# A decoder block on one core: high and low activations side by side in one matmul, the down projection with tokens stationary, one-hots built on GpSimd

## The reference, cut to what matters

```python
def block_fn(args):                      # 64 tokens at a time
    s1 = einsum('thd,kd->thk', qb[..., :half], k1); s2 = ...      # 128 keys each
    v1, i1 = top_k(s1, 16); v2, i2 = top_k(s2, 16)
    cand, cand_idx = v1[:, None] + v2[None], i1 * 128 + i2        # 256 of each head
    top, pos = top_k(cand, 16); idx = cand_idx[pos]               # 8 heads x 16 experts
    g = softmax(top)
    act = gelu(einsum('thkd,td->thk', u_tab[idx], hb)) * g
    return einsum('thk,thkd->td', act, v_tab[idx])
x = x + gt_f * rms_norm(ff, g_post_ffn)
```

## Time and profile before

| | |
|---|---|
| three runs, median (lowest to highest) | 2189.06 us (2187.78 to 2191.6) |
| the profiled execution | 2194.0 us |
| its span in the profile | 2192.2 us |
| busy: PE, PEld, DVE, ACT, POOL | 92%, 86%, 72%, 40%, 10% |
| granted TensorE clock, mean | 0.987 of 2.4 GHz |
| transfers | 618 MB, 282 GB/s on average |
| `w_lo` (L354), `w_hi` (L678) | 544 each, 1223 and 1059 ns |

### The profile page before, as it was taken

One profiled execution on the slowest core, in us unless ns is written; L12 is line 12 of the kernel. 1 busy time (PEld: TensorE's weight loads), 2 busy tenths in 40 slices (PEclk: granted clock), 3 DMA queues, 4 the chain that ended last, 5 costly groups with the idle time before them and its releaser, 6 DMA issues.

```text
span 2192.2 us, 40118 instructions
## 1 busy us (share of the span) xinstructions
PE 2017.2 (92%) x15446; PEld 1880.2 (86%) x15446; DVE 1578.6 (72%) x2251; ACT 868.2 (40%) x1272; POOL 208.5 (10%) x145
## 2 busy tenths in 40 slices
PE   5999999989999999998888888899999999999997
PEld 4888884449999999998888888898998998998996
DVE  4668997658778878866888888666666666666665
ACT  3012223025444434445555555433343333343333
POOL 0000000000000000001222222111111111111110
PEclk9999999989999999999999999999999999999999
DMA  8996666978856676666999999877777778877874
GB/s 348 422 411 242 235 231 259 393 293 309 300 167 211 209 241 213 208 197 236 339 337 339 338 337 338 316 286 287 281 279 284 283 276 285 292 266 286 293 269 147
DMA packets 135962, 618.15 MB, mean 282 GB/s; under 512 B 16049, under 2 KB 24785, under 8 KB 99025
## 3 DMA queue, kind: packets, MB, share of 16 engines
q1 hardware_dynamic: 105984, 464.57, 59.2%
q0 software_dynamic: 18496, 134.24, 16.2%
q10 hardware_dynamic: 11410, 18.36, 2.3%
HBM read 600.26 MB, written 16.79 MB: 281 GB/s over the span
## 4 chain that ended last, share of the span: by engine, by line
PE 56%; DVE 21%; issue 9%; ACT 8%; DMA 5%; DVEq 1%; ACTq 1%; SPq 0%
PE ps L936 17%; PE ps L1263 17%; DVE w_lo L354 6%; ACT w_hi L678 5%; PE ps L974 5%; DVE big L1761 5%; DVE big L1693 5%; PE ps L958 4%; PE ps L1136 4%; PE ps L1085 3%; PE ps L985 3%; ACT oh L791 2%; DVE oh L1686 1%; DVE a_lo L1738 1%; DMA early<-in_w_ada 1%
## 5 line engine op out<-in xcount | busy, mean ns | idle before, releaser
L354 DVE TENSOR_TENSOR w_lo<-raw,w_hi 128x1024 fp32r<-128x1024 f32 x544 | 662.6, 1223 | 448.4 <-ACT w_hi L678 443.9
L678 ACT ACTIVATE w_hi<-raw 128x1024 fp32r<-128x1024 f32 x544 | 576.2, 1059 | 941.8 <-PE ps L1263 452.5
L1263 PE MATMUL ps<-a_hi,w_hi 128*128 128x192 f32 x2048 | 568.7, 278 | 62.8 <-DVE w_lo L354 55.3
L936 PE MATMUL ps<-a_hi,w_hi 128*128 128x192 f32 x2048 | 572.6, 280 | 28.6 <-DVE w_lo L354 24.5
L936 PE MATMUL ps<-a_hi,w_lo 128*128 128x192 f32 x2048 | 565.0, 276 | 0.0
L936 PE MATMUL ps<-a_lo,w_hi 128*128 128x192 f32 x2048 | 565.0, 276 | 0.0
L1263 PE MATMUL ps<-a_lo,w_hi 128*128 128x192 f32 x2048 | 562.9, 275 | 0.0
L1263 PE MATMUL ps<-a_hi,w_lo 128*128 128x192 f32 x2048 | 562.9, 275 | 0.0
L1263 PEld LDWEIGHTS ps<-a_hi,w_hi 128*128 128x128 f32 x2048 | 394.4, 193 | 73.6 <-DVE w_lo L354 66.0
L936 PEld LDWEIGHTS ps<-a_hi,w_hi 128*128 128x128 f32 x2048 | 396.8, 194 | 36.0 <-DVE w_lo L354 27.5
L936 PEld LDWEIGHTS ps<-a_lo,w_hi 128*128 128x128 f32 x2048 | 396.9, 194 | 0.2 <-issue 0.2
(11 more groups left out here) (232 smaller groups left out, 2034.0 us busy)
## 6 DMA issues: line engine op xcount, KB each, us to landing
raw<-in_peer_u SPq DMA_DIRECT2D x256, 512.0 KB, 5.0
raw<-in_peer_v SPq DMA_DIRECT2D x256, 512.0 KB, 4.5
early<-in_w_ada SPq DMA_DIRECT2D x60, 1024.0 KB, 10.5
early<-in_w_front SPq DMA_DIRECT2D x42, 1024.0 KB, 9.2
raw<-in_w_ada SPq DMA_DIRECT2D x20, 1024.0 KB, 10.4
raw<-in_peer_wq SPq DMA_DIRECT2D x32, 512.0 KB, 6.6
big<-in_w_gate_f SPq DMA_DIRECT2D x16, 1024.0 KB, 5.7
raw<-in_w_front SPq DMA_DIRECT2D x14, 1024.0 KB, 8.7
```

The source lines that it names most:

```text
L354: engine.tensor_tensor(w_lo[:, s % 2, part], ring[j % ph.ring][:, part], w_hi[:, s % 2, part].bitcast(F32), ALU.subtract)\
L678: act.activation(w_hi[:, s % 2, :], ring[j % ph.ring], ACT.Copy).then_inc(hi_ready, 1)
L936: done = pe.matmul(ps[:, b % 2, 0:TD], w[:, half, k * P:(k + 1) * P], a[:, kc, 0:TD], start=kc == 0 and m == 0, stop=kc == KC - 1 and m == 2)
L1263: done = pe.matmul(ps[:, c // 2, (c % 2) * TD:(c % 2 + 1) * TD], w[:, j % 2, n * P:(n + 1) * P], a[:, blk, 0:TD], start=i is None and blk ...
```

## The change

In UP, MID and ROUTE `a_hi` and `a_lo` become one tensor `a2`, so that one matmul moves both, 384 columns, against `w_hi`; its second half of the columns collects the product with the low part. `w_lo` by the high part follows with 192 columns. When a block is done, ACT copies the second half of the columns into `stage` (`put_low`), DVE adds the first half from PSUM (`add_block`), and ACT's Gelu then works in place.

In DOWN the activations become stationary and `peer_v` moves, 512 columns at a time, so the output has tokens as rows. Tokens 0 to 127 need a high and a low stationary block; tokens 128 to 191 pack their high and low parts into one block of 128 (`second`). A unit has 10 matmuls. `a_down` lies in `a2`; the low part is written with two instructions. Row sums are made in halves of 1024 columns, one after each unit of even number. At the end `pair` adds high and low rows and the slices of `acc`.

The one-hots are made on POOL, already scaled, eight instructions of 128x128 a group, in the queue in which the gathers stand; DVE's and ACT's steps for them go. The dots are made in halves, and a part of them in MID: 14 rows in MID (5 in its first round, then 3), 50 in ROUTE (8, then 6).

```diff
-USE_FIRST, MASK_FIRST, PUT_FIRST = (5, 7, 9, 11, 13, 15), (5, 7, 9, 11, 13, 15), (7, 9, 11, 13, 15, 15)
+USE_FIRST, MASK_FIRST, PUT_FIRST = (5, 7, 9, 11, 13, 15), (4, 7, 9, 11, 13, 15), (7, 9, 11, 13, 15, 15)
 USE, MASK, PUT = (1, 4, 6, 9, 12, 14), (0, 3, 6, 8, 11, 14), (3, 6, 8, 11, 14, 15)
-DOTS_AT = (1, 2, 4, 5, 7, 9, 10, 12, 13)
-SUMS_AT = (3, 6, 11, 14)
+DOTS_MID_FIRST, DOTS_MID = tuple(range(6, 16)), (1, 4, 6, 9, 12, 14)
+DOTS_ROUTE_FIRST, DOTS_ROUTE = tuple(range(16)), (0, 1, 2, 4, 5, 6, 8, 9, 10, 12, 13, 14)
...
+SUMS_AT = (0, 2, 4, 6, 8, 10, 12, 14)
...
-        a_hi = sb("a_hi", [P, KC, T], F32R)
-        a_lo = sb("a_lo", [P, KC, T], F32R)
+        a2 = sb("a2", [P, KC * 2 * T], F32R)
+        a_pair = a2[:, :].rearrange("p (k m t) -> p k m t", m=2, t=T)
+        a_hi, a_lo = a_pair[:, :, 0, :], a_pair[:, :, 1, :]
+        a_down = a2[:, 0:8 * 2 * TD].rearrange("p (b c) -> p b c", c=2 * TD)
...
-        dots_now = sb("dots_now", [P, len(DOTS_AT)])
-        pair = sb("pair", [P, P])
+        dots_now = sb("dots_now", [P, N_ROUTE_FIRST, 2])
+        pair = sb("pair", [P, TD])
...
-            for n in range(ROWS):
+            v_rows = peer_v.rearrange("b p d -> (b p) d")
+
+            def gather_next(n):
+
+                if n >= ROWS:
+                    return
                 if n >= 3:
                     gp.wait_ge(row_used, n - 2)
                 gather(n, u_rows, got[n % 3], row_in[n % 3])
...
+            def make_masks(g):
+
+                if g == 0:
+                    gp.wait_ge(sel_made, 2)
+                else:
+                    gp.wait_ge(oh_used, g)
+                for t in range(4):
+                    token = slice(4 * g + t, 4 * g + t + 1)
+                    gp.tensor_scalar(masks[:, 0, t, :], iota[:, :], sel_T[:, 0, token], None, ALU.is_equal)
+                    done = gp.tensor_scalar(masks[:, 1, t, :], iota[:, :], sel_T[:, 1, token], sel_T[:, 2, token],
+                                            ALU.is_equal, ALU.mult)
+                done.then_inc(oh_ready, 1)
+            for n in range(3 + ROW_ROUTE_FIRST):
+                gather_next(n)
+            for it in range(PH_ROUTE.n):
+                for j in range(PH_ROUTE.per):
+                    where = MASK if it else MASK_FIRST
+                    for g in range(6):
+                        if where[g] == j:
+                            make_masks(6 * it + g)
+                    halves = DOTS_ROUTE if it else DOTS_ROUTE_FIRST
+                    row0 = ROW_ROUTE + N_ROUTE * (it - 1) if it else ROW_ROUTE_FIRST
+                    if j in halves[1::2]:
+                        gather_next(row0 + halves[1::2].index(j) + 3)
+            for n in (1, 2, 0):
+                gp.wait_ge(row_used, ROWS - (ROWS - 1 - n) % 3)
+                gather(n, v_rows, got[n], v_row_in[n])
...
-            def gelu(b0, i, per):
-
-                whole(b0, i, per)
+            def put_low(b0, i, per):
+
                 b = b0 - B_UP
+                act.wait_ge(split_used, at(i, 2 * per, 2 * b0 + 2))
                 if b % 2 == 0 and (b >= 4 or i is not None):
                     act.wait_ge(gel_out[b // 2 % 2], at(i, 4 * per, 16 * (b // 4)))
-                act.activation(stage[:, b % 4, :], ps[:, b0 % 2, 0:TD], ACT.Gelu).then_inc(gemm_evac, 1)
+                act.activation(stage[:, b % 4, :], ps[:, b0 % 2, TD:2 * TD], ACT.Copy).then_inc(low_put, 1)
+
+            def gelu(b0, i, per):
+
+                b = b0 - B_UP
+                act.wait_ge(summed, at(i, per, b + 1))
+                act.activation(stage[:, b % 4, :], stage[:, b % 4, :], ACT.Gelu).then_inc(gemm_evac, 1)
...
-            def scale_masks(g, i):
-
-                act.wait_ge(oh_masked, at(i, 6, g + 1))
-                for t in range(4):
-                    token = bass.ds(at(i, 24, 4 * g + t), 1)
-                    done = act.activation(masks[:, 1, t, :], masks[:, 1, t, :], ACT.Copy, scale=sel_T[:, 2, token])
-                done.then_inc(oh_ready, 1)
-
...
+                m, per = j // 2, ph.s_per // 2
+                if j % 2 and not (first and m == 0):
+                    put_low(ph.block + m - 1, i, per)
+                if first and m < 2:
+                    return
+                if j % 2 == 0:
+                    gelu(ph.block + m - 2, i, per)
+                elif m % 2 and not (first and m == 1):
...
             def high_group(g, i, made):
 
                 act.wait_ge(at_made, made)
                 b = 4 * (g % 2)
-                act.activation(a_hi[:, b:b + 4, 0:TD], routed_v[:, bass.ds(at(i, 8, 4 * g), 4), :], ACT.Copy)\
+                act.activation(a_down[:, b:b + 4, P:P + TD], routed_v[:, bass.ds(at(i, 8, 4 * g), 4), :], ACT.Copy)\
...
+            def put_second(b):
+
+                act.wait_ge(split_used, PH_DOWN.s_end - 1 + b // 6)
+                act.activation(f_second[:, (b - 4) * 512:(b - 3) * 512], ps[:, b, :], ACT.Copy).then_inc(f_put_act, 1)
...
+            def f_squares(tt, g):
+
+                if tt:
+                    act.wait_ge(f_paired, g + 1)
+                else:
+                    act.wait_ge(split_used, PH_DOWN.s_end - 1 + g // 2)
+                act.activation(squares[:, 4 * tt + g, :], ps[:, 4 * tt + g, :], ACT.Square, accum_out=f_ss[:, tt, g:g + 1])\
                     .then_inc(f_sq, 1)
+
+            put_second(4)
+            put_second(5)
+            f_squares(0, 0)
+            f_squares(0, 1)
+            put_second(6)
+            f_squares(0, 2)
+            f_squares(0, 3)
+            for g in range(4):
+                f_squares(1, g)
...
-                    pe.wait_ge(gemm_evac, at(i, ph.s_per // 2, b - 1))
+                    pe.wait_ge(summed, at(i, ph.s_per // 2, b - 1 - B_UP))
...
-                        for m, (w, a) in enumerate(((w_hi, a_hi), (w_hi, a_lo), (w_lo, a_hi))):
-                            done = pe.matmul(ps[:, b % 2, 0:TD], w[:, half, k * P:(k + 1) * P], a[:, kc, 0:TD],
-                                             start=kc == 0 and m == 0, stop=kc == KC - 1 and m == 2)
+                        cols = slice(k * P, (k + 1) * P)
+                        pe.matmul(ps[:, b % 2, 0:2 * TD].rearrange("p (m t) -> p m t", m=2), w_hi[:, half, cols],
+                                  a_pair[:, kc, :, 0:TD], start=kc == 0, stop=False, skip_group_check=True)
+                        done = pe.matmul(ps[:, b % 2, 0:TD], w_lo[:, half, cols], a_hi[:, kc, 0:TD], start=False,
+                                         stop=kc == KC - 1, skip_group_check=True)
...
-                    for n in range(UCH):
-                        c = (j % 2) * UCH + n
-                        for m, (w, a) in enumerate(((w_hi, a_hi), (w_hi, a_lo), (w_lo, a_hi))):
-                            done = pe.matmul(ps[:, c // 2, (c % 2) * TD:(c % 2 + 1) * TD], w[:, j % 2, n * P:(n + 1) * P],
-                                             a[:, blk, 0:TD], start=i is None and blk == 0 and c % 2 == 0 and m == 0,
-                                             stop=False, skip_group_check=True)
+                    first, low, second = (a_down[:, blk, P:2 * P], a_down[:, blk, 0:P], a_down[:, blk, 2 * P:3 * P])
+                    for tt, a, w in ((0, first, w_hi), (0, low, w_hi), (1, second, w_hi), (0, first, w_lo),
+                                     (1, second, w_lo)):
+                        for n in range(2):
+                            done = pe.matmul(ps[:, 4 * tt + 2 * (j % 2) + n, :], a, w[:, j % 2, n * 512:(n + 1) * 512],
+                                             start=i is None and blk == 0 and w is w_hi and a is not low, stop=False,
+                                             skip_group_check=True)
                     done.then_inc(split_used, 1)
...
-            def turn_out(tt, g):
...
+            pe.wait_ge(v_row_used, ROWS)
+            pe.wait_ge(pair_made, 3)
+            for g in range(4):
+                cols = slice(g * 512, (g + 1) * 512)
+                if g < 3:
+                    pe.wait_ge(f_put_act, g + 1)
+                else:
+                    pe.wait_ge(f_put_dve, 1)
+                pe.matmul(ps[:, 4 + g, :], pair[:, 0:P], acc[:, cols], start=True, stop=False, skip_group_check=True)
+                pe.matmul(ps[:, 4 + g, :], pair[:, TS:TD], f_second[:, cols], start=False, stop=True,
+                          skip_group_check=True).then_inc(f_paired, 1)
...
+                if ph in (PH_UP, PH_MID, PH_ROUTE):
+                    m = j // 2
+                    if j % 2 and (m or i is not None or ph is not PH_UP):
+                        add_block(ph.block - B_UP + m - 1, i, ph.s_per // 2)
+                if ph is PH_MID:
+                    dots_at(j, i, DOTS_MID if i is not None else DOTS_MID_FIRST, ROW_MID, 3)
+                if ph is PH_ROUTE:
+                    dots_at(j, i, DOTS_ROUTE if i is not None else DOTS_ROUTE_FIRST, ROW_ROUTE, 6)
+
+            def add_block(b, i, per):
+
+                dve.wait_ge(low_put, at(i, per, b + 1))
```

(24 more changed lines are left out.)

153 lines of the change are left out of this document (61 added, 92 removed).

## The result

The changed kernel takes 2214.5 us (median of four runs, 2212.5 to 2215.6), the kernel before 2188.4 in the same session: 1.0116 times as long, 95% interval 1.0099 to 1.0134. Forecast were 2064 us, with 1985 to 2135 as the range. The kernel did not become faster but 1.2% slower, which is small but more than the runs scatter, and the time lies outside of the range.

The account below looks back on a forecast made before the run. TensorE was taken to bound UP and MID and to set most of ROUTE and DOWN. UP -12, MID +20, DOWN -104, ROUTE -22 and the end -7 sum to -125, giving 2064 us, range 1985 to 2135.

Parts of the forecast that it names:

- one term of ROUTE: ROUTE, one-hots on POOL: each 128x128 instruction takes 0.35 us, so eight in a group take 2.8 us.
- the port's term: ROUTE: POOL waits out two-input DVE instructions, some five a group, each for half of its 1.14 us: 2.5 us.
- The idle time: ROUTE: POOL waits for DVE's half dot, about 1.1 us after TensorE's use of the group before.
- TensorE's own term in ROUTE: ROUTE: TensorE needs 38.4 us plus 2.5 for 24 one-hot matmuls, 40.9 a round if nothing waits for one-hots.
- the +10 forecast for it: First ROUTE round: all six groups stand two units apart, so it goes from about 53 to 64 us.
- POOL's instructions are dear: Rival in ROUTE: 0.5 us an instruction gives 2124, 0.94 gives 2290; chance 0.13 for 0.45 to 0.7, 0.08 above.
- UP: UP stage: a round falls from 43.7 to 40.7 us, four rounds, -12 us.
- MID: MID stage: three more rows of dots make a round 47.6 us, DVE-bound; +12, first round +8, together +20 us.
- DOWN: DOWN stage: hand-over gives 38.1 us, DVE's pieces 2.8, a round 40.9 instead of 47.4; sixteen rounds, -104 us.
- Transfers: Same bytes in less time: DOWN 327 GB/s, MID 260, ROUTE about 310, against 385 possible; nothing binds, with little room.
- The end: After the last matmul: 12 us of transposing back become about 5 us, -7 us.
- Weight loads: Rival: loads don't hide behind the wide matmul, a unit takes 3.75 us, a round 60, total 2264; chance 0.02.

Follow-up runs that it names:

- the best version: Changed kernel with one-hots back on DVE and ScalarE, a second set of one-hot buffers and two of six groups made a unit earlier: 2041.9 us, 0.9326.

## Why the prediction was wrong

**The step that failed** is one term of ROUTE: "I take 0.35, near the select, since it has the same size and one input but also reads its scalars." It is 0.69. Per group, over the 42 groups of the seven rounds (476.4 us, 11.3 each; forecast 8.0):

| | forecast | measured |
|---|---|---|
| eight instructions | 2.8 | 5.5 |
| behind DVE, and the gather | 2.5 + 1.6 | 3.7 (389.1/42 less 5.5) |
| idle between use and start | 1.1 | 2.1 (87.3/42) |

The price is 2.7 of the 3.3 us that are missing, and the run with half of the instructions puts the forecast's 2.8 in place and comes near the forecast's round. Both halves of the port's term were right: about 0.5 of a DVE piece each (0.59 us of 1.14) and some five in the way. The idle time was short by 1.0, since the gather's dot comes not 1.1 us after the use but only after a high part and a low part that wait for TensorE in turn. Taking away one of GpSimd's two waits gained nothing, as the table above shows.

**TensorE's own term in ROUTE** was too low as well, and this hid in the run with half of the instructions. "24 one-hot matmuls, 2.5" takes about 0.1 us each, but four of them, eight records, hold TensorE for 0.83 us (1295.60 to the next matmul at 1296.43; in the kernel before 1157.51 to 1158.34), 5.0 a round. So ROUTE's floor was 43.4 by the forecast's own sum and not 40.9. The version with the one-hots back on DVE has TensorE busy for 43.7 us a round, and the best version, at 46.2, stands little above it. In the run with half of the instructions GpSimd is busy for 5.6 us a group where the forecast had 6.9, and idle for 3.0 where it had 1.1, so its round of 51.8 bears out the price but not each term; that it lies so near to 50.5 is in part luck. The first round before was read too short, 53 us for 58.6 by the high parts, so of the +10 forecast for it only some 5 follow.

The rival "POOL's instructions are dear" is what happened, by its own numbers: it put the point from which the change is slower at 0.7 us, with rounds of 66 and a first of 80; measured are 0.69, 68.1 and 81.8. I gave it 0.13 up to 0.7 and 0.08 above. What misled me was the choice of the nearest row: the select and the comparison are of one size and engine, but nothing in the trace said that they cost alike. With two ends at 0.24 and 0.94 and a break-even between them, the chance of slower should have been near a half, and the range should have reached 2290.

**The clock** had no term. ROUTE's rounds show 0.85, directly at most 6.5 us a round, and it follows from the waits: 0.99 with the one-hots back.

**UP**: 41.8 for 40.7, a pair of wide and narrow matmuls every 0.285 us against 0.28. **MID**: 48.3 for 47.6, DVE-bound as said; the first round, 50.2, was already 50.3 before, so its +8 did not come. **DOWN**: 41.8 for 40.9, but for another reason. I had a hand-over of 38.1 and 2.8 of DVE's disturbances; the row sums cost 1.3 (41.8 against 40.5), and the floor is TensorE's own 39.4 (16 x 2.46), since a matmul of 512 columns takes 0.23 to 0.25 us and not 0.216. Together that gave nearly the same sum, by luck. The 0.216 was half of a record's 0.43 us in the earlier trace rows; the 16 there are eight matmuls of two records. **Transfers**: 322 GB/s in DOWN (forecast 327), 257 in MID (260), 227 in ROUTE (310, as the round is longer); landings bind nothing. **The end**: -5 for -7. Each of the eight matmuls with `pair` takes 0.86 us, 6.9 together, more than the 5 that I had for the whole. **Weight loads** hide behind the wide matmul: a unit takes 2.28 us, not 3.6. Part 3 of the Trainium skill's "TensorE: Matmul & The Clock Gate" ("What overlaps and what doesn't"), by which a load overlaps only for another row group, does not hold here.

**Left open**: why one buffer, two buffers, and gathers behind the groups all end at 68.2 or 68.3 us in the middle rounds, and what the clock costs by itself. Where the time goes is shown, to the wait for dots with two buffers, to the wait for TensorE and behind DVE with later gathers; that the sum is the same to 0.1 us is not explained. Fewer and larger instructions on GpSimd, with the one-hots left there, were not tried.

## What to carry to other kernels

An operation that moves to an engine on which the trace does not show it has no price; if the break-even lies between the two nearest rows, the forecast is open, however well the rest is worked out. Work that stood as one instruction on DVE (1.2 us for 128x1024) and four on ScalarE became eight on GpSimd (5.5 us), each of which can be caught behind a DVE instruction with two SBUF inputs. Count the instructions, and keep DVE's pieces short where GpSimd is on the path. In a loop of engines that hold each other up, a gain on one (a buffer, an earlier start) may come back as another wait or as standing still inside instructions, so look at all waits of the next engine and at its busy time together. And count instructions where the profile counts records: a time per record taken for a time per instruction was wrong here by a factor of two, twice.

## What the runs showed of the hardware that I had not expected

GpSimd needs 0.59 us for a comparison of 128x128 with one scalar per partition and 0.79 with a second step, against 0.24 between two selects of that size. Beside a stream of half-row DVE instructions it lasts 1.6 to 2.3 us in the rows shown, beside whole rows 3.3 to 4.0, while DVE's grow only from 1.22 to 1.38 or 1.46. In a dense stream a DVE piece of 1.14 us costs GpSimd 0.87. A matmul of 512 columns in fp32r with its load takes 0.23 to 0.25 us.
